# Query groups 3 to 7 and key scores of heads 2 to 7 inside the first tile's expert steps, first head ranked in one go

## What is computed

```python
def peer_ffn(x, w_query, sub_keys, expert_down, expert_up):
    def chunk(xc):                       # 128 tokens
        q = (xc @ w_query).reshape(PEER_CHUNK, PEER_HEADS, 2, half)        # 8 heads, half = 128
        s = jnp.einsum('thpk,pnk->thpn', q, sub_keys)                      # 2 x 128 key scores a head
        sv, si = lax.top_k(s, PEER_TOPK)                                   # 16 best of each 128
        cand = (sv[:, :, 0, :, None] + sv[:, :, 1, None, :])...            # 256 pairs
        top_s, sel = lax.top_k(cand, PEER_TOPK)                            # 16 experts a head
        eidx = jnp.take_along_axis(cidx, sel, axis=-1)
        g = jax.nn.softmax(top_s, axis=-1)
        u = expert_down[eidx]
        vv = expert_up[eidx]
        act = jax.nn.gelu(jnp.einsum('td,thkd->thk', xc, u), approximate=False)
        return jnp.einsum('thk,thkd->td', (g * act), vv)
```

## Time and profile before

| | |
|---|---|
| median of 3 runs | 2408.66 us (2407.15 to 2410.4) |
| the profiled execution | 2412.3 us, of which the span of its records is 2410.5 us |
| busy share of the span | PE 87%, DVE 68%, ACT 46%, POOL 34% |
| expert steps, from the first gather | about 841 to 1490 us, and 1756 to 2405 us |
| moved by gathers | 540 MB, by the weight stream 159 MB |

### The profile page before, as it was taken

The page is one execution under the profiler, slowest core; times in us unless marked ns, Lnnn a source line. Parts: engine busy times, 40 slices in busy tenths (PEclk is TensorE's granted clock), DMA queues, the critical chain, the costliest instruction groups (busy, mean ns, idle before and its releaser), DMA issues.

```text
span 2410.5 us, 32536 instructions
## 1 busy us (share of the span) xinstructions
PE 2107.4 (87%) x10192; PEld 1383.8 (57%) x10246; DVE 1640.8 (68%) x3313; ACT 1113.4 (46%) x2532; POOL 822.3 (34%) x562
## 2 busy tenths in 40 slices
PE   8999999999999988878877787999987877878877
PEld 7899899998999842222322222999852222322222
DVE  3555777777766577777777775776567777777776
ACT  5344455555544444444444444544444444444443
POOL 0000011100100066655666662010056566665663
PEclk9999999999999999999999998999999999999999
DMA  7333456655533499999999997433489999999998
GB/s 257 123 116 126 143 163 196 204 190 188 166 109 130 132 420 422 422 422 422 421 421 422 422 422 317 167 114 110 136 349 422 422 422 422 422 422 422 422 422 345
DMA packets 122844, 710.66 MB, mean 295 GB/s; under 512 B 14161, under 2 KB 16721, under 8 KB 56582
## 3 DMA queue, kind: packets, MB, share of 16 engines
q0 software_dynamic: 75264, 540.05, 54.1%
q1 hardware_dynamic: 43600, 159.12, 20.0%
q10 hardware_dynamic: 3894, 10.35, 1.2%
HBM read 708.29 MB, written 4.32 MB: 296 GB/s over the span
## 4 chain that ended last, share of the span: by engine, by line
PE 46%; DMA 31%; issue 7%; ACT 6%; DVE 5%; POOL 5%; POOLq 0%; ACTq 0%; DVEq 0%
DMA work<-in_experts,expert_idx 31%; PE ps L463 11%; PE ps L465 11%; PE ps L464 11%; PE ps L1085 6%; POOL work L930 5%; DVE work L1612 2%; PE ps L543 2%; PE ps L578 2%; PE ps L556 1%; ACT arena L1318 1%; ACT small L1315 1%; ACT L1313 1%; DVE weights_lo L448 1%; PE ps L1064 1%
## 5 line engine op out<-in xcount | busy, mean ns | idle before, releaser
L1085 PE MATMUL ps<-work,arena 128*128 128x512 f32 x2048 | 1017.2, 629 | 250.5 <-ACT arena L1318 248.9
L930 POOL DMA_INDIRECT work<-in_experts,expert_idx x512 | 778.9, 1521 | 843.7 <-issue 554.6
L1085 PEld LDWEIGHTS ps<-work,arena 128*128 128x128 f32 x2048 | 365.9, 194 | 900.1 <-ACT arena L1318 592.5
L1612 DVE CUSTOM_DVE_ANT_0 work<-h_norm,work 128x1024 f32<-128x1024 f32 x512 | 629.9, 1230 | 338.5 <-DMA work<-in_experts,expert_idx 332.0
L448 DVE TENSOR_TENSOR weights_lo<-weights,weights_hi 128x1024 fp32r<-128x1024 f32 x298 | 367.2, 1237 | 220.6 <-ACT weights_hi L443 220.4
L443 ACT ACTIVATE weights_hi<-weights 128x1024 fp32r<-128x1024 f32 x298 | 314.3, 1057 | 383.5 <-PE ps L465 363.8
L463 PE MATMUL ps<-feat_hi,weights_hi 128*128 128x256 f32 x1576 | 452.8, 287 | 7.6 <-DVE feat_lo L376 4.1
L464 PE MATMUL ps<-feat_lo,weights_hi 128*128 128x256 f32 x1576 | 447.5, 284 | 0.0
L465 PE MATMUL ps<-feat_hi,weights_lo 128*128 128x256 f32 x1576 | 447.3, 284 | 0.0
L1313 ACT ACTIVATE small<-small 128x1 f32<-128x1 f32 x512 | 103.7, 203 | 666.8 <-DVE small L1612 666.2
L463 PEld LDWEIGHTS ps<-feat_hi,weights_hi 128*128 128x128 f32 x1576 | 304.1, 193 | 12.1 <-issue 7.2
(11 more groups left out here) (174 smaller groups left out, 1785.1 us busy)
## 6 DMA issues: line engine op xcount, KB each, us to landing
weights<-in_wstream SPq DMA_DIRECT2D x298, 512.0 KB, 3.6
work<-in_experts,expert_idx POOLq DMA_INDIRECT x512
na_rows<-in_rpb POOLq DMA_DIRECT2D x32, 96.0 KB, 4.0
arena<-na_rows ACTq DMA_DIRECT2D x2, 1536.0 KB, 10.7
params<-in_par ACTq DMA_DIRECT2D x2, 1476.0 KB, 7.3
work<-bias_rows ACTq DMA_DIRECT2D x3, 512.0 KB, 6.6
params<-in_par ACTq DMA_DIRECT2D x1, 1156.0 KB, 11.7
x<-in_x SPq DMA_DIRECT2D x1, 1024.0 KB, 5.0
```

Source lines behind the costliest of these rows:

```text
L930: nc.gpsimd.indirect_dma_start(ring[:, r, :], None, experts, bass.IndirectOffsetOnAxis(ap=EIDX[:, b, c * RING + r:c * RING + r + 1], axis= ...
L1085: ins = nc.tensor.matmul(bank(2 * t + h), DIAG[:, r, :], ring[:, r, D + h * 512:D + (h + 1) * 512], start=False, stop=False)
L1612: nc.vector.tensor_tensor_reduce(ring[:, r, 0:D], HN[:, t, :], ring[:, r, 0:D], 1.0, 0.0, ALU.mult, ALU.add, hd[:, r:r + 1]).then_inc(dots ...
```

## The change

- Before the first expert step only query groups 0 to 2 are made (`PQ_FIRST = 3`), and the key scores of heads 0 and 1. ACT does the first head's exponential after group 1 rather than group 4.
- The first head's ranking runs through piece 10 (`rows`) without splits in between. Query halves 4 and 5 are split after it, 6 and 7 after piece 11.
- In the steps of tile 0, PE makes the key scores of head k + 2 after pick 1 of pass 0 of step k (k up to 5), and in steps 0 to 4 one half of query group k + 3 after pick 3 of each pass (`half_fm`). ACT copies those scores after pick 3, the group after pick 6 of pass 1, and splits one half after pick 6 of each pass. DVE splits halves after picks 1 and 3 of pass 1, in steps 0 to 3.
- DVE's wait for scores in pass 1 is for head min(k + 2, 7) instead of head 7.
- The loop over tile 0's 8 steps is written out on PE, ACT and DVE. Tile 1 keeps its loop.
- POOL's wait for the last three weight halves is gone.

```diff
--- before.py
+++ after.py
@@ -80,6 +80,8 @@
 USES = STEPS * PASSES
 PICKED = STEPS * TOPK
 ROUTES = STEPS + 1
+PQ_FIRST = 3
+PQ_MIXED = PH - PQ_FIRST
 KEYED = STEPS + 2
@@ -485,6 +487,13 @@
                                       c == chunks[0], c == chunks[-1])
                 ins.then_inc(half_done, 1)
+        def half_fm(pe, n, b, h, at=0):
+            w = split_pe(pe, n, at)
+            for c in range(KC):
+                ins = product(ps[:, b * 512 + h * S:b * 512 + (h + 1) * S], cols(w, c * P, P), feat(c, 0, S), c == 0, c == KC - 1)
+            ins.then_inc(half_done, 1)
         def half_tok(pe, n, b, h, at=0, also=None):
@@ -923,9 +932,6 @@
                         for c in range(PASSES):
                             use = l * USES + i * (2 * PASSES) + b * PASSES + c
                             for r in range(RING):
-                                if (b, c, r) == (0, 0, 2):
-                                    for n in range(L_HALF + L_HALVES - SLOTS, L_HALF + L_HALVES):
-                                        wait_alone(pool, w_landed[n % SLOTS], At(l, L_HALVES).landed + 16 * (n // SLOTS + 1), pool_passed)
                                 wait_alone(pool, slot_used[r], use + 1, pool_passed)
                                 nc.gpsimd.indirect_dma_start(
                                     ring[:, r, :], None, experts,
@@ -1066,28 +1072,56 @@
                                                    PAR[:, Q_KEYS + s * NKEY:Q_KEYS + (s + 1) * NKEY], start=True, stop=True)
                     ins.then_inc(sc_done, 1)
-                for j in range(L_PQ):
+                def pq_free(j):
                     if j >= 2:
                         pe.wait_ge(lproj_taken, l * N2 + L_PROJ + L_GATE + j - 1)
+                for j in range(PQ_FIRST):
+                    pq_free(j)
                     group_fm(pe, G_LAYER + LG_PQ + j, 6 + j % 2, at, also=(
                         lambda c: c % 2 or pe.wait_ge(n_peer.hT, l * 4 + c // 2 + 1)) if j == 0 else None)
                     if j != 1:
                         key_scores(max(j - 1, 0))
-                key_scores(PH - 1)
-                for t in range(TT):
+                def slot(t, use, r):
+                    pe.wait_ge(diag_ready, use * RING + r + 1)
+                    for h in range(2):
+                        ins = nc.tensor.matmul(bank(2 * t + h), DIAG[:, r, :], ring[:, r, D + h * 512:D + (h + 1) * 512],
+                                               start=False, stop=False)
+                    ins.then_inc(slot_used[r], 1)
+                def opened(t):
                     for h in range(2):
                         nc.tensor.matmul(bank(2 * t + h), ZERO[:, 0:P], ZERO[:, :], start=True, stop=False)
...
+                def closed(t):
...
+                opened(0)
+                for k in range(PH):
+                    j = PQ_FIRST + k
+                    for c in range(PASSES):
+                        for r in range(RING):
+                            slot(0, l * USES + k * PASSES + c, r)
+                            if (c, r) == (0, 1) and k + 2 < PH:
+                                key_scores(k + 2)
+                            if r == 3 and j < PH:
+                                if c == 0:
+                                    pq_free(j)
+                                half_fm(pe, G_LAYER * 2 + 2 * (LG_PQ + j) + c, 6 + j % 2, c, at)
+                closed(0)
+                for t in range(1, TT):
+                    opened(t)
+                    with pe.Fori(0, PH * PASSES) as i:
+                        for r in range(RING):
+                            slot(t, l * USES + i + t * PH * PASSES, r)
+                    closed(t)
         @block.scalar
@@ -1286,38 +1320,58 @@
                     nc.scalar.activation(SC[:, 0:STEPS, :, :].rearrange("p (t h) s n -> p t h (s n)", h=PH)[:, :, h, :],
                                          bank(4 + h % 2).rearrange("p (t n) -> p t n", t=TT), ACT.Copy).then_inc(sc_ready, 1)
-                for j in range(L_PQ):
-                    n = 2 * (LG_PQ + j) + SLOTS
-                    if n < L_HALVES:
-                        split_hi(act, L_HALF + n, at)
+                def take_query(j):
                     act.wait_ge(half_done, at.halves + L_HALF + 2 * (LG_PQ + j) + 2)
                     nc.scalar.activation(pqT[:, 2 * j:2 * j + 2, :], bank(6 + j % 2).rearrange("p (t n) -> p t n", t=TT),
                                          ACT.Copy).then_inc(lproj_taken, 1)
-                    if n + 1 < L_HALVES:
-                        split_hi(act, L_HALF + n + 1, at)
-                    if j != 1:
+                def hi_query(q):
+                    if q < 2 * L_PQ:
+                        split_hi(act, L_HALF + 2 * LG_PQ + q, at)
+                for j in range(PQ_FIRST):
+                    hi_query(2 * j + SLOTS)
+                    take_query(j)
+                    hi_query(2 * j + 1 + SLOTS)
+                    if j == 1:
+                        gate_exp(0)
+                    else:
                         take_scores(max(j - 1, 0))
-                    if j == 4:
-                        gate_exp(0)
-                take_scores(PH - 1)
-
-                for t in range(TT):
+                def step_act(k, b, mixed=None):
+                    act.wait_ge(gates_ready, l * ROUTES + k + 1)
+                    for c in range(PASSES):
+                        for r in range(RING):
+                            pick = l * PICKED + k * TOPK + (c * RING + r + 1)
+                            act.wait_ge(dots_ready, pick)
...
+                            if (c, r) == (0, 4):
+                                gate_exp(k + 1)
+                            if mixed:
+                                mixed(c, r)
+                for k in range(PH):
+                    def mixed(c, r):
+                        j = PQ_FIRST + k
+                        if (c, r) == (0, 3) and k + 2 < PH:
+                            take_scores(k + 2)
+                        if r == 6 and j < PH:
+                            if c:
+                                take_query(j)
+                            hi_query(2 * j + SLOTS + c)
+                    step_act(k, k % 2, mixed)
+                for t in range(1, TT):
                     with act.Fori(0, PH // 2) as i:
                         for b in range(2):
...
+                            step_act(i * 2 + (t * PH + b), b)
         @block.vector
@@ -1578,44 +1632,58 @@
                     return sums, first, second, split, matched, taken, rows, gates
                 ch.step(nc.vector.memset(SC[:, STEPS:KEYED, :, :], 0.0))
-                split_lo(dve, L_HALF + 2 * LG_PQ + SLOTS, at)
+                def lo_query(q):
+                    if q < 2 * L_PQ:
+                        split_lo(dve, L_HALF + 2 * LG_PQ + q, at)
+                lo_query(SLOTS)
                 wait_alone(dve, sc_ready, l * PH + 1, dve_passed)
                 ch.sync()
-                nxt = 2 * LG_PQ + SLOTS + 1
                 rc = Chain(dve, route_step)
                 for n, piece in enumerate(keyed(rc, 0) + paired(rc, 0, 0)):
                     piece()
-                    if n in (1, 3, 5, 7, 9):
-                        for m in range(nxt, min(nxt + 2, L_HALVES)):
-                            split_lo(dve, L_HALF + m, at)
-                        nxt += 2
-                for m in range(nxt, L_HALVES):
-                    split_lo(dve, L_HALF + m, at)
+                    if n == 10:
+                        lo_query(4)
+                        lo_query(5)
+                lo_query(6)
+                lo_query(7)
                 wait_alone(dve, sc_ready, l * PH + 2, dve_passed)
                 for piece in keyed(rc, 1):
                     piece()
                 rc.restart()
-                for t in range(TT):
+                def step_dve(t, k, b, uses, mixed=None):
+                    rc = Chain(dve, route_step)
+                    pairs = paired(rc, k + 1, 1 - b, l * PICKED + k * TOPK + 1)
+                    for c in range(PASSES):
+                        use = uses + c
+                        if c:
+                            if t == 0:
+                                wait_alone(dve, sc_ready, l * PH + min(k + 3, PH), dve_passed)
+                            halves = keyed(rc, k + 2)
+                        for r in range(RING):
+                            dve.wait_ge(g_landed[r], use * 16 + 16)
+                            nc.vector.tensor_tensor_reduce(ring[:, r, 0:D], HN[:, t, :], ring[:, r, 0:D], 1.0, 0.0,
+                                                           ALU.mult, ALU.add, hd[:, r:r + 1]).then_inc(dots_ready, 1)
+                            if c == 0:
+                                pairs[r]()
+                            elif r % 2 == 0:
+                                halves[r // 2]()
+                            elif mixed:
+                                mixed(r)
+                    rc.restart()
```

(7 more changed lines are left out.)

46 lines of the change are left out of this document (6 added, 40 removed).

## The result

The changed kernel takes 2397.75 us (median of 5, 2395.1 to 2398.37) beside 2409.55 for the kernel before: a ratio of 0.9948, interval 0.9934 to 0.9963, so 11.8 us less. A second set on another chip gave 2398.4, ratio 0.9951 (0.9937 to 0.9964). The forecast was 2394, 14.8 us less, a ratio of 0.9939, which both intervals still hold: the 3 us between them are not clear of noise. The profiles read the terms of the sum more sharply, and two of them were well off.

The account below looks back on a forecast made before the run. The gather stream, full at 421 GB/s, bounds the expert steps, so the first gather's moment counts. 42.0 - 24.7 - 2.0 - 0.5 = 14.8 us off the profiled 2412.3; as a median 2394 us, 8-in-10 range 2388 to 2404.

Parts of the forecast that it names:

- Part 1: Ranking of head 0 in one go: first gather 21.0 us earlier in each layer, 42.0 us gross gain.
- Part 2: Weights sharing the gather stream: 19 more halves behind the first gather at 1.3 us each, 24.7 us lost.
- Part 3: Start of the expert steps: slot 0 reused near 844 us, 1 us lost in each layer, bounds 0 and 4.
- the stock: Start of the steps: 8 ring gathers and 4 weight halves keep the stream fed about 25 us, until 846.
- the cover: Start of the steps: margin of 2 us between slot 0's reuse near 844 and the stream running dry at 846.
- Part 4: Work inside mixed steps: PE needs 40.8 us against the stream's 42.4, so the added work costs nothing.
- The rival in which PE becomes the bound: Mixed steps: dearer half groups or slots make PE the limit, for example 2435 us; chance 0.13.
- Part 5: Written-out loop and POOL's removed wait: perhaps 0.4 MB more code, 0.5 us lost; the wait nothing.
- the first gather: Sign at the start of layer 0's steps: near 820 us, with the ranking ended 1 us before.
- layer 1: Sign: its expert steps, first gather to last, about 12 to 14 us longer than before.
- PE's 40 of 42 us: Sign in a mixed step: PE busy nearly 40 of 42 us, still waiting now and then for ACT.
- the dips below 400 GB/s: Sign against the prediction: it is wrong if the stream shows such dips after step 0.

Follow-up runs that it names:

- h: Changed kernel, but layer 1's first three weight halves load only after layer 0's sums are done: 2395.05 us, 0.9939 of the kernel before.
- b: Changed kernel with a quarter of the columns loaded of each weight half that falls into the steps: 2384.8 us, 0.9897 of the kernel before.
- d: Changed kernel with 100 idle matmuls on PE ahead of its first slot, in both layers: 2418.2 us, 1.0033 of the kernel before.
- j: Changed kernel with 34 idle matmuls on PE between group 2 and slot 0, to keep its clock up: 2399.3 us, 0.9954 of the kernel before.
- e: Changed kernel with tile 1's loops written out too on PE, ACT and DVE: 2407.8 us, 0.9988 of the kernel before.
- c_pe_load28: Changed kernel with 28 idle matmuls on PE behind each half group of the mixed steps: 2440.9 us, 1.0131 of the kernel before.
- after: The changed kernel itself, 2397.75 us; run and profiled a second time beside other variants, 2398.4 us.
- a_rank_alone: Kernel before with only head 0's ranking done in one go, all query groups still ahead of the steps: 2428.1 us, 1.0078 of the kernel before.
- f: Changed kernel with weight half 4 split ahead of the ranking: 2393.4 us, 0.9935 of the kernel before.

## Why the prediction was right, and where it was not

- **Part 1, 42.0 us gross.** 21.02 and 21.01 us. Right.
- **Part 2, 1.3 us a half.** Measured 1.30 in the stream, and h gave back 1.3 to 1.8 a half. Right, and b and h show that the halves carry the larger part of what the layers grew by. The earlier trace rows was the better of the two rows, because there the mixture is that of the steps.
- **Part 3, the start.** The account had slot 0 at 844 with the stock ending at 846. It came at 840.36: 1.6 of it is the earlier start, and a weight half was waited for only 1.10 us. The loss was 0 and not 1 us a layer; d shows the stream dry from about 846, and j and e that it can suffer some us before that. On the clock, the rows of group 2 (817 to 823):

```profile
817.00:819.00 2.00, 0.57 (x2) 0.57 (x3) 1.99 (x3) 0.00 (x0) 0.61 (x1) 0.50 0.00 0
819.00:821.00 2.00, 2.00 (x12) 2.00 (x11) 1.94 (x4) 0.00 (x0) 1.70 (x2) 0.50 0.60 223
821.00:823.00 2.00, 2.00 (x14) 2.00 (x14) 0.00 (x0) 0.00 (x0) 1.70 (x2) 0.71 0.80 221
```

  After 6.5 us idle PE starts at 1.2 GHz, and the group takes 7.7 us (818.4 to 826.1, when ACT can copy it) in place of 5.76; the third row, at 0.71, has the return to 2.4 GHz. The Trainium skill, "TensorE: Matmul & The Clock Gate", section "Part 1: The HAM clock gate", has both, the fall and the return, and the trace agrees. The prediction had let the whole group run at the half clock, 11.5 us, and that is most of the rest by which slot 0 came early. Layer 0 of j shows that the gap cost nothing here, since it lay inside the cover.
- **Part 4, the work inside the steps.** "Nothing" was right, the need of 40.8 us behind it was not: it is 34.5, measured 36 busy. The term that was mis-sized is the slot, 2.11 us where it is 1.72. The rival in which PE becomes the bound thus had 8 us of air and not 1.6; its chance of 0.13 was too high, while its slope (ten times each us above 42.4) is confirmed by c_pe_load28.
- **Part 5, the written-out loop, 0.5 us.** This is the term that failed. The bytes were forecast well: 0.36 MB more within the layers (0.29 in the whole kernel, 24 packets) against 0.4. Their price was not: bytes at the mean rate gave 0.5, the ends and the dips of the change's own layers come to 5 to 6 us net of a dip of before (below), and writing out the other tile cost 9.2 us with 22 packets. The bound that I took from the rows ended at 1 us, since I priced a block of code as if all 16 engines shared it. No run has the change with tile 0's loop kept, so its own price of the code is read from the profile and not measured.

  The Trainium skill, "Runtime: NRT & Kernel Launch", section "Instruction fetch mechanics", calls a boundary of a 16 KiB block mostly hidden and prefers unrolled code. The packets of one code queue agree on the size (1.05 MB in 64, 16 KB each); those of the other are mostly of 8 KB. On the cost the runs decide otherwise: beneath a full stream, unrolling was the dearer form.

**Where the missing 3 us are.** The layers grew by 29.9 us; the 19 halves at 1.30 are 24.7 of it. Of the other 5.2, the longer end of the stream has about 2.7 us in layer 0 and 2.2 in layer 1. In tile 1, after has two short dips in layer 0 and one in layer 1, such as this one, which cost about 1.2 us a layer:

```profile
1184.00:1188.00 4.00, 4.00 (x11) 1.84 (x10) 3.40 (x8) 0.90 (x4) 2.05 (x2) 1.00 0.99 385
```

The share is 0.99, so the transfer engines are busy in a dip and don't stand idle for lack of gathers; nor do the records have a code packet within 8 us of it. The kernel before and a_rank_alone have no such dips in tile 1, c_pe_load28 has none, and the others have them in at least one layer (the second profile of after has none in layer 0). Against these stands a dip of about 1.5 us that the kernel before had at the start of layer 1. In the 8 us behind the first gather the stream moved less than before in layer 0 (268 GB/s against 306, 0.7 us) and more in layer 1 (329 against 236, 1.8 us). So 4.9 + 2.4 - 1.5 + 0.7 - 1.8 = 4.7 us are named for 5.2 that are sought, which is as near as sums over stretches of 1 to 4 us come. With the start's 2 us not spent, this gives the shortfall: -2.0 on the start, +5.2 for the end and the dips less 0.5 forecast, 2.7 in the layers.

Of the signs that the prediction named for itself, the first gather (818.38), slot 0 and layer 1 (12.4 us longer for 12 to 14) came as said. PE's 40 of 42 us did not, layer 0 grew by 17.5 for 14 to 16, and the dips below 400 GB/s, which were to show it wrong, were there. They cost 1 to 1.5 us a layer, too little to turn the result.

**What stays open.** The runs agree that the long end and the dips need mixed steps at the full stream, and e that more code makes the end longer. That the code sits on one transfer engine, which then stays behind, is argued, not shown: the records name no engine. For it: the tail at one sixteenth of the share, its absence in c_pe_load28, where the stream has slack, and that the 0.25 MB more of code that e moves within its two layers than after, at the rate of one engine (421 / 16 = 26.3 GB/s), are 9.5 us, where 9.2 were measured (which may be luck, as 3 of e's us lie behind ACT's late copy). Against it: by the same price the change itself, with 0.36 MB more than before within the layers, should have lost 14 us, and no more than 6 can be found. How the dips arise is open too, as are ACT's late copy in e and j and the 3 us between the layers in f.

## What to carry to other kernels

When a stream is the bound, date its first transfer and price what is moved behind that date by its share of the stream in a row where both already mix; moving the start forward pays only if whatever frees the buffers is moved forward with it. Take an engine's time per unit from rows at one clock, long after a gap, or its spare time comes out wrong by a factor (here 1.6 us a step for 8). Under a full stream count code as a load of its own kind: writing out a loop cost 9 us here with a quarter of a megabyte. And before a surplus is put down to one cause, look in the profile where it lies: a third of those 9 us lay elsewhere than at the code.

## What was not expected of the hardware

- Writing out a loop, with 22 more packets of code, 0.24 MB, cost 9.2 us beneath a stream of 420 GB/s, while 0.52 MB of small loads in pieces of 512 B cost about 2.
- The end of the stream takes 5 to 6 us after steps with this code at 420 GB/s, and 3 after the same code at 378 (c_pe_load28).
- At the end of a stream 0.06 of the share, 25 GB/s, can go on for 3 us, the share of one of 16 transfer engines.
- Six to eight gathers of 1 MB queued ahead did not hold a weight load back as long as themselves: 8 to 9 us to landing at the start, 7.9 in the mixed steps, where a gather took 15.9 (3.7 is the median load of the whole kernel).
- A stream can be slow with its engines busy: after more than 5 us at nothing, 20 us at 360 to 406 GB/s followed with a share of 0.97 to 1.00, and a dip in tile 1 has 0.99 with 385.
